# Attention stage: weight panels loaded one stage earlier, and a pair loop with a lag of one instead of two

## The reference

```
def attention_mixer(h, w_qkv, q_g, k_g, w_o, rope):
    qkv = h @ w_qkv                       # 256x1024 @ 1024x1536
    q, k, v = split(qkv)                  # 16 query heads, 4 key/value heads, 64 wide
    q = axial_rope(rmsnorm(q, q_g), rope)
    k = axial_rope(rmsnorm(k, k_g), rope)
    s = einsum(q, k) * scale              # each query head against its group's keys
    p = softmax(s)
    o = einsum(p, v)
    return o @ w_o                        # 256x1024 @ 1024x1024
```

## Time and profile before

| what | value |
|---|---|
| median of 3 runs | 2693.67 us (2690.18 to 2694.2) |
| the profiled execution | 2693.67 us, its span 2692.1 us |
| busy share of the span | PE 80%, PEld 49%, DVE 61%, ACT 28%, POOL 39% |
| attention stage | about 18 to 143 us of the span |
| attention, 60 to 110 us | PE 30.45, DVE 31.85, ACT 29.54 us busy of 50 |

### The profile page before, as it was taken

How to read it: one execution, slowest core, us unless ns; L and a number is a source line. 1 busy time by engine, 2 the same in 40 slices (tenths; PEclk the granted TensorE clock), 3 DMA queues, 4 the chain that set the end, 5 groups by cost and what they waited for, 6 DMA issues and landing times. The chain is left out here.

```text
span 2692.1 us, 24931 instructions
## 1 busy us (share of the span) xinstructions
PE 2157.3 (80%) x8403; PEld 1327.3 (49%) x8403; DVE 1635.7 (61%) x3138; ACT 755.3 (28%) x1537; POOL 1053.5 (39%) x1121
## 2 busy tenths in 40 slices
PE   6789989999799878777767666799788867777775
PEld 5578847788597564322222222587554322222221
DVE  6578845688656565646564754565564765566554
ACT  4444444544355121211111101354112111101110
POOL 0010010011002046666666666020356666666664
PEclk9899989999899989998999899899899889999988
DMA  7178822488644488999999999834579999999997
GB/s 253 48 266 299 318 83 102 165 321 314 230 167 147 154 315 328 360 370 371 367 365 384 350 375 372 298 132 172 217 282 372 361 377 361 360 386 366 356 370 279
DMA packets 244425, 774.81 MB, mean 288 GB/s; under 512 B 20361, under 2 KB 24873, under 8 KB 244322
## 3 DMA queue, kind: packets, MB, share of 16 engines
q0 software_dynamic: 160512, 587.27, 57.8%
q1 hardware_dynamic: 83810, 186.25, 19.4%
HBM read 772.35 MB, written 1.10 MB: 287 GB/s over the span
## 5 line engine op out<-in xcount | busy, mean ns | idle before, releaser
L2648 PE MATMUL experts_fourth<-experts_v_slot,experts_diagonal 128*128 128x512 f32 x960 | 478.5, 629 | 211.2 <-DMA experts_v_slot<-in_expert_v_dram,experts_at 114.2
L2648 PE MATMUL experts_first<-experts_v_slot,experts_diagonal 128*128 128x512 f32 x1024 | 505.1, 642 | 153.1 <-issue 81.4
L2283 POOL DMA_INDIRECT experts_v_slot<-in_expert_v_dram,experts_at x512 | 485.0, 947 | 355.2 <-issue 135.7
L2648 PEld LDWEIGHTS experts_fourth<-experts_v_slot,experts_diagonal 128*128 128x128 f32 x960 | 171.4, 196 | 518.4 <-issue 477.2
L2648 PEld LDWEIGHTS experts_first<-experts_v_slot,experts_diagonal 128*128 128x128 f32 x1024 | 200.2, 204 | 442.9 <-issue 417.9
L2278 POOL DMA_INDIRECT ring<-in_expert_u_dram,experts_at x368 | 346.9, 943 | 143.1 <-issue 105.8
L2422 DVE CUSTOM_DVE_ANT_0 ring<-ring,experts_second 128x1024 f32<-128x1024 f32 x192 | 230.1, 1219 | 204.7 <-DMA ring<-in_expert_u_dram,experts_at 189.1
L2422 DVE CUSTOM_DVE_ANT_0 ring<-ring,experts_third 128x1024 f32<-128x1024 f32 x176 | 207.7, 1218 | 97.9 <-DMA ring<-in_expert_u_dram,experts_at 93.3
L538 POOL DMA_DIRECT2D mlp_ada_half<-in_w_ada_dram x48 | 36.2, 755 | 531.8 <-DVE csum L659 308.2
L2532 ACT ACTIVATE experts_dots<-experts_dots 128x16 f32<-128x16 f32 x32 | 6.9, 215 | 731.0 <-issue 413.9
L179 DVE TENSOR_TENSOR mix_lo<-ring,mix_hi 128x1024 fp32r<-128x1024 f32 x96 | 132.1, 1383 | 126.6 <-ACT mix_hi L2017 126.5
(11 more groups left out here) (407 smaller groups left out, 3987.1 us busy)
## 6 DMA issues: line engine op xcount, KB each, us to landing
mlp_ada_half<-in_w_ada_dram POOLq DMA_DIRECT2D x48, 1024.0 KB, 6.7
ring<-in_w_in_dram SPq DMA_DIRECT2D x20, 2048.0 KB, 8.3
ring<-in_mlp_w_in_dram SPq DMA_DIRECT2D x16, 2048.0 KB, 10.4
ring<-in_mlp_w_out_dram SPq DMA_DIRECT2D x16, 2048.0 KB
ring<-in_w_query_dram SPq DMA_DIRECT2D x8, 2048.0 KB, 8.1
ring<-in_gla_w_in_dram SPq DMA_DIRECT2D x6, 2048.0 KB, 8.2
ring<-in_w_out_dram SPq DMA_DIRECT2D x4, 2048.0 KB, 7.9
experts_v_slot<-in_expert_v_dram,experts_at POOLq DMA_INDIRECT x512
```

Of the source, the lines that this page charges most:

```text
L2283: pool.indirect_dma_start(v_slot[:, j % VS, :], None, rows_v, bass.IndirectOffsetOnAxis(ap=at[:, n, j:j + 1], axis=0)).then_inc(v_in[j % V ...
L2648: mm = pe.matmul(y[n // PH][:, b, :], diagonal[n % 2][:, j, :], v_slot[:, j % VS, b * HALF:(b + 1) * HALF], start=n % PH == 0 and j == 0, ...
```

## The change

All of it is in the attention stage and in the loads ahead of it.

The norm stage ahead of attention issues four panels (`w_qkv` 0, 2, 1 and `w_o` 0) where it issued two, and attention issues only `w_o` 1 itself (its argument `own_panels` is gone). `rope_tables` runs on DVE after low part 3 instead of after low part 6. Square and root of group 2 run on ACT after high part 14 instead of 15, and its means on DVE after low part 14. Group 2 is turned in the banks of `more` (0 and 1) instead of `sums`, ahead of score(3), waits for the exponentials of two pairs instead of three, and score(3) waits for it to be moved in. In the pair loop the lag shrinks by one: PE does score(pair), transposes(pair-1), weigh(pair-2); ACT does exponentials(pair), move(pair-1), high(pair-2); DVE does maximum(pair), normalise(pair-1), take(pair-2).

```diff
@@ attention, SP
-                start_panels(sp, K, own_panels, split_done, panels[0])
@@ attention, PE
         def turned_bank(g, t):
-            return sums[:, 1, t, :] if g == 2 else more[:, 2 * g + t, :]
+            return more[:, (0, 2, 0)[g] + t, :]
...
                     if g == 2:
-                        pe.wait_ge(exp_done, 4 * 3)
+                        pe.wait_ge(exp_done, 4 * 2)
...
-                    if pair == 4:
+                    if pair in (3, 4):
                         pe.wait_ge(moved_in, 3 * T)
...
                 score(0)
                 score(1)
+                transposes(0)
                 for pair in range(2, PAIRS):
-                    score(pair)
-                    transposes(pair - 2)
                     if pair == 3:
                         turn_in(2)
-                    if pair >= 3:
-                        weigh(pair - 3)
-                transposes(PAIRS - 2)
-                weigh(PAIRS - 3)
+                    score(pair)
+                    transposes(pair - 1)
+                    weigh(pair - 2)
@@ attention, ACT
                     split(p)
-                    if p == 6:
-                        square(0)
-                        root(0)
-                    if p == 15:
-                        square(2)
-                        root(2)
+                    if p in (6, 14):
+                        square(p // 4 - 1)
+                        root(p // 4 - 1)
...
-                exponentials(0)
-                exponentials(1)
-                for pair in range(2, PAIRS):
+                for pair in range(PAIRS):
                     exponentials(pair)
-                    move(pair - 2)
-                    if pair == 3:
+                    if pair >= 1:
+                        move(pair - 1)
+                    if pair >= 2:
+                        high(pair - 2)
+                    if pair == 2:
                         move_in(2)
-                    if pair >= 3:
-                        high(pair - 3)
-                move(PAIRS - 2)
-                high(PAIRS - 3)
@@ attention, DVE
                     lower(p)
-                    if p == 6:
+                    if p == 3:
                         rope_tables()
...
-                means(2)
+                    if p == 14:
+                        means(2)
                 maximum(0)
                 maximum(1)
                 normalise(0)
                 scaled(2)
+                maximum(2)
                 normalise(1)
-                maximum(2)
                 rotate(2)
+                take(0)
                 for pair in range(3, PAIRS):
+                    maximum(pair)
                     normalise(pair - 1)
-                    maximum(pair)
-                    if pair >= 4:
-                        take(pair - 4)
+                    take(pair - 2)
                 normalise(PAIRS - 1)
-                for pair in range(PAIRS - 4, PAIRS):
-                    take(pair)
+                take(PAIRS - 2)
+                take(PAIRS - 1)
@@ block_one
-    norm(nc, K, gain(0, 0), hT=hT, panels=wide(w_qkv, (0, 2)))
-    attention(nc, K, A, memory, gain(1, 0), own_panels=wide(w_qkv, (1,)),
-              out_panels=wide(w_o, range(2)), following=pairs(0, range(2)))
+    norm(nc, K, gain(0, 0), hT=hT, panels=wide(w_qkv, (0, 2, 1)) + wide(w_o, range(1)))
+    attention(nc, K, A, memory, gain(1, 0), out_panels=wide(w_o, range(1, 2)), following=pairs(0, range(2)))
```

More of the change, by code:

```diff
@@ L1334, in _, with attention @@
                 tail.vector(dve, own)
-def attention(nc, K, A, memory, gain, own_panels, out_panels, following):
+def attention(nc, K, A, memory, gain, out_panels, following):
     PANELS, PIECES_IN, ALL, BUFFERS = 3, 12, 20, 4
```

## The result

The changed kernel takes 2719.98 us (median of 4 runs, 2716.45 to 2724.68) against 2693.22 us of the kernel before in the same session: ratio 1.0102, 95% interval [1.0085, 1.012]. The forecast was 2711 us, 17.2 more than before, with a range to 2720, thus to +26.3; measured is +26.8, just outside. The sign came out as written, and so did the waits; one term, the clock, was priced too low. The trace of the changed kernel has the first output piece 22.9 us late, where the sum said 17.2.

What follows compares the result with a forecast made beforehand. The prediction took attention's pair loop as bound by a ring of waits on DVE and ACT, no engine full. Its terms 6.5 + 6.7 + 4 = 17.2 us on 2693.67 gave 2711 us, range 2699 to 2720.

Steps and rivals of the forecast that it cites:

- Part 1: Loads ahead of attention: the rope table lands late behind more panels, DVE waits, PE's piece 7 starts late; +6.5 us.
- The queue's order: DMA queue ahead of attention: the table stays behind the panels issued before it, landing at 37.6 us.
- rival A: DMA queue: the table passes the panels, leaving 1.6 us of the loads' cost; +12.3, 2706 us; chance 0.13.
- Parts 2 and 3: Attention pairs: later start and longer steady loop with PE in its ring, less a shorter drain; +6.7 us.
- start: First pairs of attention: exp of pair 0 at 66.7 instead of 65.46, exp of pair 3 +4.2 us.
- ring: Steady pair loop: chain of waits from one pair to the next, now through PE, 6.07 us instead of 4.78.
- B: Pair loop: no slower, PE's ring paid back elsewhere and the clock holds; 6.5 us alone, 2700; chance 0.10.
- D: Pair loop: faster with exp out of the ring, 5.9 us less, 2688; chance 0.05.
- Part 4: PE's clock in the pair loop: granted clock falls, 3.07 us of PE per ring become 3.8; +4 us over five rings.
- rival C: PE in the pair loop: low clock holds most of the loop, +10 instead of +4, 2717 us; chance 0.11.
- the 0.80: Granted PE clock assumed for the new pair loop, taken between 1.00 and 0.77 seen before.

Runs made afterwards that it cites:

- the fillers: Changed kernel plus twelve unused transposes per pair from pair 1, ahead of PE's wait for the normalised pair: 2549.18 us against 2559.50 for the changed kernel.
- both halves of part 1: Kernel before with the panel loads moved forward and rope_tables behind low part 3, attention loop as before: 2698.15 us, ratio 1.0013.
- the loads alone: Kernel before with only the four panel loads moved forward, rope_tables still behind low part 6: 2697.76 us, ratio 1.0022 to before.

## Why the prediction was too low

- **Part 1**, the loads and the table: +6.5 forecast, +5.55 measured. The chain from the panels over the table to DVE and PE was right; the table landed 0.9 us earlier, mostly because it followed the fourth panel by 2.6 and not by 3.4 us. Its issue was reckoned at 21.2 and came at 25.52, which did no harm to the sum, since the landing was added up from the panels' landings and not from the issue. The queue's order held, so rival A is out: 7.1 us behind its issue would have been 32.6. The Trainium skill's sentence that the time to initiate a DMA is usually small beside the DMA (DMA: Bandwidth & Descriptors, "Issuing engines are not separate DMA queues") does not hold here for a small transfer either, which the prediction did not see: the issue of 32 KB took 4.41 of the 13.4 us to its landing.
- **Parts 2 and 3**, start, ring and drain at the clock of the prediction: +6.7 forecast. Measured: exp of pair 0 +1.13 (72.14 - 65.46 - 5.55), and from there to the first output piece 49.56 us with the fillers against 43.90 before, +5.66; together +6.8. Link by link it is +4.4 up to exp of pair 3 (forecast +4.2), +3.2 for the four rings (+3.4) and -0.9 for the drain, the stretch from exp of pair 7 to the first output piece (-0.8). The last is partly luck: before's drain of 8.66 us held groups at the low clock, and in the kernel with both halves of part 1, where they ran at the high one, it took 7.26, less than the 7.79 with the fillers. Rivals B and D are out: the ring of 6.04 is PE's and is paid in full.
- **Part 4**, the clock, is the step that failed: +4 forecast. From exp of pair 0 to the first output piece the changed kernel takes 60.09 us and the one with fillers 49.56: +10.5. The four rings hold 7.3 of it (31.49 against 24.17), the start 1.4 and the drain 1.8. 5.55 + 6.8 + 10.5 = 22.9. The sum had 3.1 for the four rings and 0.8 for everything outside them. This is the case of rival C (+10, since each burst follows a gap of 2.9 us), to which I gave 0.11.

Where the 4 us went wrong is not mainly the 0.80, since 0.75 was granted. I divided PE's 3.07 us by the mean clock of a window, which gives 4.1 us at 0.75: 1.0 more a ring, where 1.83 more was measured. A window's mean counts the idle time too, and in this loop the low level falls on the work: at a mean of 0.75 between full and half clock, half of a ring of 7.87 us is low, 3.9 us. In the slowest ring some 5.8 us of work at the low clock cost 2.73, so a loss of 1.83 stands for about 3.9 us of such work, an estimate: all of the low time. Ring by ring, groups over their length at the high clock: from 98.81 it is 0.57 + 0.89 + 0.12 = 1.58, and 6.04 + 1.58 = 7.62 of 7.63 measured; from 113.87 it is 0.88 + 0.90 + 0.95 = 2.73, and 8.77 of 8.75; the other two fit within 0.01 as well. The three groups are in the ring, so each is paid whole. In the Trainium skill (TensorE: Matmul & The Clock Gate, "A second HAM failure mode"), short idles between groups of matmuls make the clock swing and cost throughput. The runs agree, and give the size: 1.83 us a ring, gone when twelve transposes cut the idle of 2.87 us to 1.41.

The prediction named the rows from 60 to 80 for this, where the idles are 5.3 us long. A nearer case stood in before's trace, in the drain:

```profile
103.69 1.06 PE L1476 MATMUL attn_more<-ident,mod 128*128 128x128 f32 x8 [2.70 <-ACT shared L1586]
104.68 1.85 PE L1489 MATMUL attn_sums<-shared,attn_v 128*64 128x256 f32 x8
106.46 1.95 PE L1476 MATMUL attn_more<-ident,mod 128*128 128x128 f32 x8
```

After an idle of 2.70 us the groups take 1.85 and 1.95 us, while behind the loop's idles of 1.39 to 1.63 they kept to 1.06 to 1.14. The same stretch of the kernel with both halves of part 1 stayed high after an idle of 2.70 (1.08, 1.06), so the clock does not fall each time.

The medians put the loss at 26.8 and 23.5 us, the traces at 22.9 and 25.7 at the first output piece. A trace is one execution and a median several; what parts them was not followed further.

## What to carry to other kernels

Where TensorE is on the ring with an idle stretch in it, price its groups at their low-clock duration one by one, not by a window's mean clock. That gives an upper bound: here 2.73 us a ring, of which the four rings lost 1.40 to 2.73, two thirds in the mean. Before reordering two instructions on one engine, write the ring with every engine's queue in it, the small instructions too: a take of 0.34 us that waits behind a move set a ring of 6.29. Here the loads moved forward delayed every small transfer behind them in the queue; a wait for such a one belongs behind the work that others need.

## What the runs showed of the hardware that was not expected

- TensorE ran faster for being given more: twelve transposes a pair that nobody needs, 1.53 us of added work, took the ring from 7.87 (mean) to 6.04 us, the granted clock from 0.77 to 1.00, and the whole kernel down by 10.3 us.
- An issue on SP stood 4.41 us for 32 KB with four panels issued ahead of it, though SP had stood 0.9 us at the stage's barrier; before it took 0.34. In the kernels with both halves of part 1 and with the loads alone it took 4.40 and 4.41.
- The same program took 2693 us in one group and 2537 in another, on another chip. From 1000 to 1600 us, in the gather of the experts, the columns of the earlier trace rows for before (first line, one chip) and for the changed kernel (second, another chip):

```profile
1000.00:1600.00 600.00, 444.77 (x977) 182.21 (x975) 360.65 (x867) 93.12 (x278) 392.41 (x416) 0.94 0.96 362
```
```profile
1000.00:1600.00 600.00, 472.39 (x1089) 192.23 (x1088) 392.02 (x937) 106.51 (x319) 433.63 (x460) 0.99 1.02 403
```

362 against 403 GB/s; the changed kernel moved 358 on the first. Each group ran on one chip in one session, so the runs don't part the two, and why the second moves more was not tried.
